# A two-layer decoder kernel: the router worked by token halves, the norm's root moved from the one-hots to the expert slots, and the first gather cut into chunks

## The chip, the cores and the metric

The kernel runs on one core of one Trainium2 chip. The metric is the device time of one execution in microseconds (us), and the time given is the median of three runs.

## The reference, cut to what matters

The model has two layers. Each adds a mixer (attention or a recurrence) to `x` and then a mixture of experts. There are 256 tokens of width 1024, 32 experts in 4 groups of 8, and an expert has 512 hidden columns. All is float32.

```
x += Mixer(RMSNorm(x))
x += HierMoE(RMSNorm(x)):
    g_logits = h @ wg_r + bg_r              # 4 groups, the best one is taken
    e_in     = (h @ we_r + be_r)[that group]
    top_v, top_i = top_k(e_in, 2)           # two experts of the group
    gate = softmax(g_logits)[best] * softmax(top_v)
    y[token] = sum over its two experts of gate * (silu(h @ w_gate[e]) * (h @ w_up[e])) @ w_down[e]
RMSNorm(x) = x * rsqrt(mean(x * x) + eps) * gain
```

## The kernel before, in words

The weights of the experts are read once per layer, 32 experts x 3 matrices x 2 MB. They pass through twelve places of 2 MB in the on-chip memory (`places`; a unit is what one place holds). All loads are issued by the SP queue in one fixed order. A load waits until the unit that was in its place is used up, which TensorE (PE) tells by the semaphore `unit_used`. `load_unit` (L366) does this for one unit and `load_matrices` (L385) for four at a time. Eight rounds ("quads") follow, with four experts each: a gate, an up and a down matrix, each of four units. In the first gate matrix of a layer (`QUARTERED`) a unit holds a quarter of the rows for all four experts, so that it is free after a quarter of the matrix. While PE goes through the end of the mixer and the router, SP has the first twelve units loaded and then has to wait.

Each engine's instructions are written out by hand in its own order. Around the router they are these:

- PE: the output projection (`project_out`, L1105), into it set the transposes of `x` (`turn_x`, L962). Token half 0 is transposed at once. The first columns of half 1 (`turn_x(pe, layer, 1, 0)`) wait for `added` to count VectorE's first addition for that half. The last four matmuls of the projection stand behind these transposes, and their end frees the last place for unit 5. Then `route_and_experts` (L1140) follows: two strips of partial logits, the logits, the copies of x into four PSUM banks (`start_sums`, which the experts' results are later added to), two matmuls that only keep the array at work (`keep_busy`), the ranks (how many earlier tokens chose the same expert), and `moe_pe`.
- VectorE (DVE): `finish_mixer` (L1539) adds the projection to `x`, half 0 whole and half 1 in two parts. It makes the mean squares, asks ScalarE for `exp(-0.5 ln v)`, and refines this by four small steps (`inverse_root`, L849). `route` (L1582) then makes the scores of both halves. Every pair of experts in a group is compared ("duels"), the two best of the best group are `picked`, and with the ranks one-hot matrices `sel` are made (`placed`, L790), which are multiplied by the root of each token (L799).
- ScalarE (ACT): `finish_mixer` (L1363) squares x, copies transposed x out of PSUM (`keep_xT`, L969), and takes the root (`take_root`, L861).

In `moe_pe` (L569) PE gathers the tokens of 4 experts x 32 slots by matmuls with `sel` (L577). Of the first quad, chunks 0 to 3 are gathered ahead of the gate matrix and chunks 4 to 7 behind its first quarter (`gather_rest`).

An engine takes its instructions in order. `turn(...)` and `and_wait(...)` put a wait for an instruction's own end behind it.

Of the kernel before, what the change touches and what calls it, by code (L numbers as in the profile page):

```python
# [92 lines left out]
ROOTS = ((2, 2), (20, 8), (28, 8), (2, 2), (2, 2), (44, 16), (44, 16), (44, 8), (2, 2))  # L93
# [47 lines left out]
def build(nc, t, where, const_width, stop_after=4):  # L141
    with ExitStack() as ctx:
# [118 lines left out]
        over_i = sb("over_i", [P, 2], I32)  # L261


        names = ["small_landed", "tables_landed", "sums_started", "in_half_landed", "begin_landed", "begin_second", "begin_third", "begin_fourth", "gains_landed", "xt_first_landed", "xt_second_landed", "xt_third_landed", "even_dims", "odd_dims", "gather_begun", "xT_begun", "half_landed", "x_first_landed", "x_second_landed", "first_landed", "pos_landed", "lb_landed", "router_landed", "masks0_landed", "masks_landed", "consts_landed", "filler_ready", "unit_used", "stored",
# [8 lines left out]
                 "strips", "strips_kept", "last_strips_kept", "logits_done", "group_max", "group_exp", "top_diff", "top_exp", "picked_ready", "ranks_done",  # L273
# [294 lines left out]

        def moe_pe(pe, layer, over, rnd):  # L569
# [4 lines left out]
            def gather_chunks(a, b, bank=None):  # L574
                for c in range(a, b):
                    for tc in range(TC):
                        mm = pe.matmul(psum[:, YB + c // 4 if bank is None else bank, (c % 4) * P:(c % 4 + 1) * P], x[:, tc, c * P:(c + 1) * P],  # L577
                                       sel[:, tc, :], start=tc == 0, stop=tc == TC - 1)
                return mm

            def gather(chunks=KC // 2):
                for half in range(2):
                    gather_chunks(4 * half, 4 * half + chunks).then_inc(m["gathered"], 1)

            def gather_rest():
                gather_chunks(4, 8).then_inc(m["gathered"], 1)
                pe.wait_ge(m["xT_ready"], 1)
# [20 lines left out]
            def matrix(i, matrix, out, inp, rows, width, halfway=lambda: None, quarterway=lambda: None):  # L608
# [7 lines left out]
                for c in range(rows - per if last else rows):  # L616
                    if c == rows // 2:
                        halfway()
                    if c == rows // 4:
                        quarterway()  # L620
# [18 lines left out]
            pe.wait_ge(m["sel_ready"], n17 + 1)  # L639
            if over:  # L640
                pe.wait_ge(m["y_ready"], 2 * n16)
# [1369 lines left out]
```

## Time and profile before

| | us |
|---|---|
| median of 3 runs | 1168.25 |
| lowest, highest | 1167.83, 1169.03 |
| profiled execution, its own time | 1166.55 |
| its span | 1164.8 |
| PE busy | 876.4 (75%) |
| DVE busy | 223.8 (19%) |
| ACT busy | 126.7 (11%) |
| DMA queue q1, share of the 16 engines | 91.0% |
| HBM read | 445.61 MB, 383 GB/s over the span |

The profiled execution took 1166.55 us, of which 1164.8 us is the span from its first to its last recorded event, so 1.75 us lie around the span. Layer 0's router stands at 157 to 180 us of the span and layer 1's at 722 to 745 us. Busy shares are averages over stages that have different limits.

### The profile page before, as it was taken

The page shows a single profiled execution, that of the slowest core. Times are in us where ns is not written, and L with a number is a line of the kernel's source. Part 1 is how long each engine was busy: PE and PEld are TensorE (multiplying, and loading weights), DVE is VectorE, ACT ScalarE, POOL GpSimd, SP SyncE. Part 2 cuts the span into 40 slices and gives each one's busy share as a digit, 9 for nine tenths or more (in the row PEclk, how much of TensorE's full clock was granted, in tenths as well). Part 3 has the DMA queues.
Part 4 walks back from the last instruction along what each step waited for, and adds up shares of the span by engine and source line. Part 5 has one row for each costly group of instructions (what it writes and reads, how often), then busy time and mean ns, then how long its engine had stood idle before and what let it go on. Part 6 is the DMA issues. An engine that isn't in the chain of part 4 may idle for free.

```text
span 1164.8 us, 11459 instructions
## 1 busy us (share of the span) xinstructions
PE 876.4 (75%) x5104; PEld 394.0 (34%) x5104; DVE 223.8 (19%) x470; ACT 126.7 (11%) x249; POOL 0.5 (0%) x5
## 2 busy tenths in 40 slices
PE   8999999747474738485899999977474747474776
PEld 7555554212121212121246655433131313131312
DVE  2732332010101010101127541410000101000001
ACT  3411311000000000000021431200000000000000
POOL 0000000000000000000000000000000000000000
PEclk9999999888888877777999999998787878788889
DMA  9776659999999999999996477899999999999997
GB/s 347 304 321 257 267 219 378 430 435 433 435 433 433 435 433 435 435 430 414 424 423 284 154 293 276 317 441 433 433 435 435 433 435 433 433 430 432 417 426 308
DMA packets 19637, 447.45 MB, mean 384 GB/s; under 512 B 2560, under 2 KB 2816, under 8 KB 5504
## 3 DMA queue, kind: packets, MB, share of 16 engines
q1 hardware_dynamic: 19584, 446.67, 91.0%
q8 instruction: 43, 0.70, 0.2%
q14 instruction: 10, 0.08, 0.0%
HBM read 445.61 MB, written 1.05 MB: 383 GB/s over the span
## 4 chain that ended last, share of the span: by engine, by line
DMA 56%; PE 42%; DVE 1%; another core or an unknown queue 1%; issue 0%; ACT 0%; SPq 0%; DVEq 0%
DMA places<-in_together 47%; PE psum L631 14%; PE psum L1016 11%; DMA places<-in_quarters 8%; PE psum L1117 5%; PE psum L1013 4%; PE psum L577 1%; PE psum L1029 1%; PE psum L1057 1%; PE psum L565 1%; DMA places<-in_w_in 0%; PE psum L1144 0%; PE psum L698 0%; PE psum L968 0%
## 5 line engine op out<-in xcount | busy, mean ns | idle before, releaser
L631 PE MATMUL psum<-places,mixed 128*32 128x512 f32 x3040 | 421.8, 707 | 276.3 <-DMA places<-in_together 249.2
L631 PEld LDWEIGHTS psum<-places,mixed 128*32 128x32 f32 x3040 | 110.4, 127 | 570.5 <-issue 448.7
L1016 PE MATMUL psum<-places 128*128 128x512 f32 x288 | 126.3, 593 | 0.0
L1016 PEld LDWEIGHTS psum<-places 128*128 128x128 f32 x288 | 53.6, 190 | 61.4 <-issue 61.2
L577 PEld LDWEIGHTS psum<-sel,x 128*128 128x128 f32 x528 | 60.4, 192 | 17.0 <-issue 15.1
L577 PE MATMUL psum<-sel,x 128*128 128x128 f32 x528 | 64.3, 279 | 1.7 <-DVE sel L799 1.7
L565 PE MATMUL psum<-y_sb,spread 128*128 128x512 f32 x128 | 59.6, 606 | 2.1 <-ACT y_sb L768 1.4
L820 DVE TENSOR_TENSOR sig<-psum,sig 128x512 f32<-128x512 f32 x16 | 11.1, 692 | 253.4 <-ACT sig L760 253.4
L823 DVE TENSOR_TENSOR mixed<-psum,sig 128x512 f32<-128x512 f32 x16 | 11.1, 692 | 245.4 <-PE psum L631 245.4
L833 DVE COPY y_sb<-psum 128x512 f32<-128x512 f32 x14 | 9.7, 692 | 180.2 <-PE psum L631 180.2
L762 ACT COPY mixed<-psum 128x512 f32<-128x512 f32 x16 | 9.4, 586 | 320.6 <-PE psum L675 320.6
L1013 PE MATMUL psum<-places 128*128 128x256 f32 x192 | 42.9, 381 | 0.0
L1013 PEld LDWEIGHTS psum<-places 128*128 128x128 f32 x192 | 36.1, 190 | 5.7 <-issue 1.0
L760 ACT ACTIVATE sig<-psum 128x512 f32<-128x512 f32 x16 | 9.6, 597 | 255.9 <-PE psum L631 255.9
L565 PEld LDWEIGHTS psum<-y_sb,spread 128*128 128x128 f32 x128 | 22.8, 189 | 38.6 <-issue 33.7
L768 ACT COPY y_sb<-psum 128x512 f32<-128x512 f32 x16 | 9.4, 586 | 209.2 <-PE psum L631 181.8
L1117 PE MATMUL psum<-places,y_sb 128*128 128x512 f32 x64 | 28.2, 594 | 0.7 <-ACT small L1396 0.7
L1117 PE MATMUL psum<-places 128*128 128x512 f32 x64 | 28.5, 592 | 0.0
L826 DVE TENSOR_TENSOR mixed<-psum,consts 128x512 f32<-128x512 f32 x32 | 21.9, 690 | 31.8 <-PE psum L577 31.8
L1117 PEld LDWEIGHTS psum<-places,y_sb 128*128 128x128 f32 x64 | 11.9, 190 | 14.8 <-issue 13.9
L1388 ACT ACTIVATE places<-psum,small 128x512 f32<-128x512 f32 x16 | 10.1, 684 | 57.7 <-PE psum L1016 53.6
L1117 PEld LDWEIGHTS psum<-places 128*128 128x128 f32 x64 | 11.8, 190 | 13.4 <-issue 13.4
(252 smaller groups left out, 505.4 us busy)
## 6 DMA issues: line engine op xcount, KB each, us to landing
places<-in_singles SPq DMA_DIRECT2D x32, 2048.0 KB, 10.1
places<-in_quarters SPq DMA_DIRECT2D x22, 2048.0 KB, 35.1
places<-in_w_in SPq DMA_DIRECT2D x12, 2048.0 KB, 26.7
places<-in_w_out SPq DMA_DIRECT2D x4, 2048.0 KB, 14.3
places<-in_quarters SPq DMA_DIRECT2D x4, 1024.0 KB, 45.6
places<-in_w_in SPq DMA_DIRECT2D x2, 1024.0 KB, 27.2
places<-in_w_in SPq DMA_DIRECT2D x3, 512.0 KB, 8.7
x<-in_x SPq DMA_DIRECT2D x2, 512.0 KB, 13.6
```

Of the source, the lines that this page charges most:

```text
L565: mm = pe.matmul(psum[:, ACC + 2 * n + tc, :], spread[:, tc, :], y_sb[:, 512 * n:512 * (n + 1)], start=False, stop=False, skip_group_check ...
L577: mm = pe.matmul(psum[:, YB + c // 4 if bank is None else bank, (c % 4) * P:(c % 4 + 1) * P], x[:, tc, c * P:(c + 1) * P], sel[:, tc, :], ...
L631: mm = pe.matmul(psum[slots, out + n, :], inp[:, c, slots], slot(layer, unit)[:, at + 512 * n:at + 512 * (n + 1)], start=c == 0, stop=c == ...
L820: turn(nc.vector.tensor_tensor(sig, psum[:, GATE, :], sig, ALU.mult))
L823: nc.vector.tensor_tensor(flat(act_h), psum[:, UP, :], sig, ALU.mult).then_inc(m["act_ready"], 1)
L826: nc.vector.tensor_tensor(xT[:, 4 * half:4 * half + 4, :], psum[:, 6 + half, :].rearrange("p (c s) -> p c s", s=P), gain_cols[:, 2 + layer ...
L1013: mm = pe.matmul(banks[:, m // 2, (m % 2) * SEQ:(m % 2 + 1) * SEQ], w[:, c, m * P:(m + 1) * P], hT[:, c, :], start=c == 0, stop=c == KC - 1)
L1016: mm = pe.matmul(banks[:, m, :], hT[:, c, m * P:(m + 1) * P], w[:, c, :], start=c == 0, stop=c == KC - 1)
L1029: mm = pe.matmul(psum[:, 4 + m, 0:SEQ], w[:, c, m * P:(m + 1) * P], hT[:, c, :], start=c == 0, stop=c == KC - 1)
L1057: mm = pe.matmul(banks[:, m, :], hT[:, c, m * P:(m + 1) * P], w[:, c, :], start=c == 0, stop=c == KC - 1)
L1117: return pe.matmul(psum[:, OUT_BANK[layer] + 2 * tc + n, :], mixT(half)[:, c, tc * P:(tc + 1) * P], w[:, c, 512 * n:512 * (n + 1)], start= ...
L1388: r = nc.scalar.activation(dst[:, tc * 512:(tc + 1) * 512], proj(g)[:, tc, :], function, scale=small[:, 2 + tc:3 + tc])
```

## The change

It does the following in both layers.

1. The root of token half 0 is asked for and refined right behind the first addition (`ask_root`, `refine_root` in DVE's `finish_mixer`), ahead of DVE's additions for half 1. ACT takes it behind its first `keep_xT`. The root of half 1 is asked for at the end and refined within the duels of half 0.
2. Scores, duels, picks, ranks and the first `sel` are made by token halves, each with a signal of its own.
3. `sel` is no longer multiplied by the roots. A matmul of `sel` with the roots gives one number per slot (`scale_slots`), ACT copies it to `slot_scale`, and it scales the sigmoid and both products of an expert.
4. The first gather goes by chunks: chunk 0 and chunk 1 ahead of the gate matrix, and the others ahead of its rows 2, 3 and 5 (`go_on_gathering`).
5. The matmuls for the largest expert count (`count_picked`) and all four `start_sums` go behind or into the first gate matrix, and the two `keep_busy` matmuls go.
6. `value_load` of the count on PE is put behind the loop over the quads.

The diff, cut to its core:

```
         def moe_pe(pe, layer, over, rnd):
+            def scale_slots(bank):
+                for tc in range(TC):
+                    mm = pe.matmul(psum[:, bank, SEQ:SEQ + 1], sel[:, tc, :], small[:, 2 + tc:3 + tc], start=tc == 0, stop=tc == TC - 1)
+                return mm
...
+            def begin_gather():
+                pe.wait_ge(S["sel_first"], layer + 1)
+                gather_some(0, 1, YB + 1, (0,))
+                gather_some(1, 2, YB, (0,))
+                pe.wait_ge(m["sel_ready"], 1)
+                gather_some(0, 1, YB + 1, (1,)).then_inc(S["gather_begun"], 1)
+                gather_some(1, 2, YB, (1,))
+                scale_slots(YB).then_inc(S["gather_begun"], 1)
+
+            def go_on_gathering(c):
+                begun = 3 * layer
+                if c == 0:
+                    pe.wait_ge(S["xT_begun"], begun + 1)
+                elif c == 1:
+                    pe.wait_ge(S["xT_begun"], begun + 2)
+                elif c == 2:
+                    gather_some(2, 4, YB + 1, range(TC)).then_inc(m["gathered"], 1)
+                    count_picked(pe)
+                    pe.wait_ge(m["xT_ready"], 1)
+                elif c == 3:
+                    gather_some(4, 6, YB, range(TC)).then_inc(S["gather_begun"], 1)
+                elif c == 4:
+                    pe.wait_ge(S["xT_begun"], begun + 3)
+                elif c == 5:
+                    gather_some(6, 8, YB + 1, range(TC)).then_inc(m["gathered"], 1)
+                elif c == 6:
+                    pe.wait_ge(m["xT_ready"], 2)
...
                 if first:
-                    pe.wait_ge(S["xT_begun"], layer + 1)
+                    matrix(0, 0, GATE, xT, KC, FF, each_chunk=go_on_gathering)
+                    start_sums(pe, layer, (0, 1, 2, 3))
+                    pe.wait_ge(S["route_ready"], layer + 1)
...
             def one_hots(quad):
-                placed(sel, quad)
-                nc.vector.tensor_tensor(sel, sel, small[:, 2:4].unsqueeze(2).broadcast_to([P, TC, P]),
-                                        ALU.mult).then_inc(m["sel_ready"], 1)
+                placed(sel, quad).then_inc(m["sel_ready"], 1)
...
-                nc.scalar.activation(sig, psum[:, GATE, :], ACT.Sigmoid).then_inc(m["sig_ready"], 1)
+                nc.scalar.activation(sig, psum[:, GATE, :], ACT.Sigmoid, scale=slot_scale).then_inc(m["sig_ready"], 1)
                 act.wait_ge(m["turned"], n16 + i + 1)
                 nc.scalar.copy(actT, psum[:, GATE, :].rearrange("p (c s) -> p c s", c=FC))
+                keep_scale(UP)
...
@@ TensorE, route_and_experts
-                logits(0)
+                logits(0).then_inc(S["logits_done"], 1)
                 pe.wait_ge(S["xT_third"], layer + 1)
                 strips(1, range(KC // 2, KC)).then_inc(S["strips"], 1)
-                start_sums(pe, layer, (0,))
                 pe.wait_ge(S["last_strips_kept"], layer + 1)
                 logits(1).then_inc(S["logits_done"], 1)
-                start_sums(pe, layer, (1, 2, 3)).then_inc(S["sums_started"], 1)
-                keep_busy(pe, 2, 7, ident, consts[:, 0:SEQ])
...
+                pe.wait_ge(S["picked_ready"], TC * layer + 1)
+                pe.matmul(psum[:, 4, 0:32], before, picked[:, 0, :], start=True, stop=True).then_inc(S["ranks_done"], 1)
+                pe.wait_ge(S["scores_read"], layer + 1)
+                pe.matmul(psum[:, 5, 0:32], ones[:, 0:P], picked[:, 0, :], start=True, stop=False)
+                pe.wait_ge(S["picked_ready"], TC * layer + 2)
+                pe.matmul(psum[:, 5, 0:32], before, picked[:, 1, :], start=False, stop=True).then_inc(S["ranks_done"], 1)
                 moe_pe(pe, layer, 0, 0)
@@ ScalarE, finish_mixer
                 keep_xT(layer, 0, slice(0, 2), nc.scalar.copy).then_inc(S["xT_first"], 1)
+                take_root(act, turn)
                 for half, signal in enumerate(("xT_second", "xT_third")):
@@ VectorE, finish_mixer
                 V.memset(rank.rearrange("p c e -> p (c e)"), 0.0)
+                ask_root(mean_square(dve, layer, 0), 2, 1)
+                refine_root(dve, turn)
                 dve.wait_ge(S["out_second"], layer + 1)
                 V.tensor_tensor(x[:, 1, 0:512], x[:, 1, 0:512], sums(1)[:, 0:512], ALU.add).then_inc(S["added"], 1)
...
                 keep_strips(0, V.tensor_copy).then_inc(S["strips_kept"], 1)
-                norm_root(dve, turn, 2 * layer + 1)
+                dve.wait_ge(S["squares"], SQUARES[2 * layer + 1])
+                turn(V.tensor_tensor(small[:, 1:2], small[:, 1:2], small[:, 7:8], ALU.add))
+                ask_root(mean_square(dve, layer, 1), 3, 1)
@@ VectorE, route
+                def duels(tc):
...
+                    turn(V.tensor_tensor(by_duel, ..., ALU.subtract))
+                    if tc == 0:
+                        refine_root(dve, turn)
+                    turn(V.tensor_tensor(by_row, by_row, ..., ALU.is_gt))
+                    turn(V.tensor_reduce(beaten_by[:, tc]..., by_duel, AX, ALU.add))
+                    turn(V.tensor_scalar(g_hot[:, tc], ..., 1.0, None, ALU.is_lt))
+                    and_wait(dve, V.scalar_tensor_tensor(by_group(picked[:, tc]), ...), S["picked_ready"], TC * layer + tc + 1)
...
+                scores(0)
+                duels(0)
+                scores(1)
+                V.memset(small[:, 60:61], 0.0).then_inc(S["scores_read"], 1)
+                duels(1)
+                place_first(0).then_inc(S["sel_first"], 1)
+                place_first(1).then_inc(M[layer]["sel_ready"], 1)
```

## Rows read from the trace of the kernel before

**Rows 1.** From the page, part 2: tenths of the clock and GB/s in 40 slices.

```profile
PEclk9999999888888877777999999998787878788889
GB/s 347 304 321 257 267 219 378 430 435 433 435 433 433 435 433 435 435 430 414 424 423 284 154 293 276 317 441 433 433 435 435 433 435 433 433 430 432 417 426 308
```

**Rows 2.** The chain that ended last: start us, us, what.

```profile
192.63 28.94 DMA places<-in_together
221.62 9.86 PE psum L631 x64
...
763.02 7.20 PE psum L631 x64
...
1097.94 8.59 PE psum L631 x64
```

**Rows 3.** The timeline of SP's queue, layer 0's router: start us, us, engine, line.

```profile
164.59 3.47 SPq L369 DMA_DIRECT2D places<-in_singles  x2
```

**Rows 4.** Stretches: length, busy per engine, then granted clock, DMA share, GB/s.

```profile
176.00:177.00 1.00, 1.00 (x13) 0.58 (x15) 0.00 (x0) 0.73 (x4) 0.00 (x0) 1.00 0.09 33
179.00:180.00 1.00, 1.00 (x12) 1.00 (x11) 0.93 (x4) 0.00 (x0) 0.00 (x0) 1.00 1.30 246
182.00:192.00 10.00, 10.00 (x100) 2.99 (x92) 0.69 (x1) 0.60 (x1) 0.00 (x0) 1.00 1.03 441
```

**Rows 5.** Timeline, end of layer 0's projection: start us, us, engine, line, operation.

```profile
159.84 0.69 DVE L1549 TENSOR_TENSOR x<-x,psum 128x512 f32<-128x512 f32 x1 [2.05 <-PE psum L1117]
160.72 1.01 ACT L974 COPY places<-psum 128x1024 f32<-128x1024 f32 x1 [1.90 <-PE psum L968]
...
162.24 0.60 PE L968 MATMUL psum<-consts,x 128*128 128x128 f32 x4
...
164.59 0.69 DVE L1551 TENSOR_TENSOR x<-x,psum 128x512 f32<-128x512 f32 x1 [4.06 <-PE psum L1117]
...
165.51 0.66 PE L968 MATMUL psum<-consts,x 128*128 128x128 f32 x4
...
166.20 0.59 ACT L974 COPY places<-psum 128x512 f32<-128x512 f32 x1 [0.17 <-PE psum L968]
...
167.16 0.16 DVE L856 TENSOR_TENSOR small<-small 128x2 f32<-128x2 f32 x1 [0.72 <-ACT small L867]
```

**Rows 6.** The same timeline, the router's scores, duels, picks and one-hots.

```profile
166.68 0.42 PE L1149 MATMUL psum<-both_strips,mixed 128*128 128x40 f32 x2
...
169.00 0.43 DVE L1602 SCALAR_TENSOR_TENSOR mixed<-psum,small,consts 128x40 f32<-128x40 f32 x2 [1.08 <-PE psum L1149]
...
169.46 0.82 DVE L1605 TENSOR_TENSOR mixed<-mixed 128x640 f32<-128x640 f32 x1
...
172.24 0.23 DVE L1611 SCALAR_TENSOR_TENSOR picked<-mixed 128x64 f32<-128x64 f32 x1
...
173.51 0.43 DVE L793 TENSOR_TENSOR sel<-consts,rank 128x256 f32<-128x256 f32 x1
```

**Rows 7.** The same timeline, PE's copies of x, gather and first expert matmuls.

```profile
168.72 2.82 PE L558 MATMUL psum<-x,consts 128*128 128x512 f32 x6
...
174.45 2.05 PE L577 MATMUL psum<-sel,x 128*128 128x128 f32 x16 [0.86 <-DVE sel L799]
...
176.44 1.92 PE L631 MATMUL psum<-places,mixed 128*32 128x512 f32 x16
...
180.27 12.22 PE L631 MATMUL psum<-places,mixed 128*32 128x512 f32 x112
```

**Rows 8.** Stretches of the expert stages, for the clock; columns as in Rows 4.

```profile
215.50:220.00 4.50, 0.00 (x0) 0.00 (x0) 0.00 (x0) 0.00 (x0) 0.00 (x0) 1.00 1.08 466
989.75:991.50 1.75, 0.00 (x0) 0.00 (x0) 1.41 (x3) 0.52 (x1) 0.00 (x0) 1.00 0.95 412
991.75:993.00 1.25, 0.00 (x0) 0.00 (x0) 0.00 (x0) 0.00 (x0) 0.00 (x0) 0.50 0.97 419
1149.00:1155.00 6.00, 3.98 (x30) 1.29 (x28) 0.00 (x0) 0.00 (x0) 0.00 (x0) 1.00 0.84 352
```

More of the change, by code:

```diff
@@ L606, in over_matrix, with matrix @@
                     mm.then_inc(m["used"], 1)
-            def matrix(i, matrix, out, inp, rows, width, halfway=lambda: None, quarterway=lambda: None):
+            def matrix(i, matrix, out, inp, rows, width, halfway=lambda: None, each_chunk=lambda c: None):
                 if over:
@@ L711, in moe_pe @@
             y_all = 2 * QUADS
+            count = pe.value_load(over_i[0:1, layer:layer + 1], min_val=0, max_val=SEQ)
             with pe.If(count > SLOTS):
@@ L771, in act_quad @@
                     nc.scalar.copy(y_sb[:, 512:1024], psum[:, YB + 1, :]).then_inc(m["y_ready"], 1)
-            keep_gathered(n17 + 1, first=not over)
+            if over:
+                keep_gathered(n17 + 1)
+            else:
+                begin_gathered()
             with act.Fori(0, QUADS if over else QUADS - 1) as i:
@@ L847, in build, with ask_root @@
         roots_asked, roots_taken = [], []
-        def inverse_root(dve, instruction, turn, col, count):
+        def ask_root(instruction, col, count):
             assert ROOTS[len(roots_asked)] == (col, count)
@@ L853, in inverse_root, with refine_root @@
             instruction.then_inc(S["root_in"], 1)
+        def refine_root(dve, turn):
+            col, count = roots_asked[-1]
             dve.wait_ge(S["root_out"], len(roots_asked))
@@ L859, in inverse_root @@
             turn(nc.vector.tensor_tensor(v, y, z, ALU.mult))
+        def inverse_root(dve, instruction, turn, col, count):
+            ask_root(instruction, col, count)
+            refine_root(dve, turn)
         def take_root(act, turn):
@@ new lines, in route, with scores @@
+                n_rows = SCORES // PER_GROUP
+                each = [P, n_rows, PER_GROUP, PER_GROUP]
+                by_group = lambda a: a.rearrange("p (g e) -> p g e", g=N_GROUPS)
+                def scores(tc):
+                    dve.wait_ge(S["logits_done"], TC * layer + tc + 1)
+                    turn(V.scalar_tensor_tensor(rt[:, 64 + tc * SCORES:64 + (tc + 1) * SCORES], psum[:, 4 + tc, SEQ:SEQ + SCORES],
+                                                small[:, 2 + tc:3 + tc], rb[:, layer, :], ALU.mult, ALU.add))
@@ new lines, in place_first @@
+                def place_first(tc):
+                    dve.wait_ge(S["ranks_done"], 3 * layer + tc + 1)
+                    turn(V.scalar_tensor_tensor(rank[:, tc, 0:32], psum[:, 4 + tc, 0:32], 1.0, picked[:, tc], ALU.add, ALU.mult))
+                    return V.tensor_tensor(sel[:, tc].rearrange("p (e s) -> p e s", e=TILE),
+                                           const("iota").unsqueeze(1).broadcast_to([P, TILE, SLOTS]),
+                                           rank[:, tc, 0:TILE].unsqueeze(2).broadcast_to([P, TILE, SLOTS]), ALU.is_equal)
```

156 lines of the change are left out of this document (73 added, 83 removed).

## The prediction

> **What bounds the kernel now.** Four views in turn. The page first: in 40 slices the DMA rate stands at 430 to 441 GB/s in slices 7 to 18 and 26 to 38 and falls to 154 between, so that the expert stages are bound by loads and the mixers are not [rows 1]. The chain of waits next: behind layer 0's first quad it goes over from PE to the four-unit load issued at 192.63 us, and from there each quad is a load with a short PE piece behind it [rows 2]. A load stream that never runs dry ends a fixed time after it begins. So the question is when it begins, and the stretches answer it: unit 5 is issued at 164.59 [rows 3], the DMA runs dry soon after 176.0 (33 GB/s in that us), and it is at work again in the us from 179.0 (246 GB/s), then at 441 GB/s throughout [rows 4]. What starts it is the end of the first quarter of the first gate matrix, which frees a place: 176.44 + 1.92 = 178.36 [rows 7]. I call this moment Q. Earlier than the dry point nothing is won, but Q may come some 2 us earlier with full gain. The last view is the timeline from the end of the projection to Q, and every edit is priced by what it does to Q. Layer 1 has the same instructions in the same order, so each term counts twice.
>
> **1. DVE's early root adds a wait (+1.57 us).** The root of half 0 needs ACT, and ACT takes it behind its first copy of transposed x, which starts at 160.72 [rows 5]. In the kernel before, a copy started at 166.20 and DVE's first refining step at 167.16, 0.96 later. This copy is 1.01 long where that one was 0.59, so the step comes 1.38 after 160.72, at 162.10 [rows 5]. Four steps at 0.20 (0.16 and the gap of the wait behind each) end at 162.89. DVE stands still from about 159.1 until then, and queued behind the waiting instruction is the first addition of half 1, which ran at 159.84 [rows 5]. It now runs 162.89 to 163.58. PE waits for it: a transposition follows an addition by 165.51 - 164.59 - 0.69 = 0.23, so this one begins at 163.81 instead of 162.24 [rows 5]. The rest of the projection stands behind it in PE's order, then the second addition, the strips, the logits, and in SP's queue units 5 and 6. All move by 1.57. The bounds are 0 (ACT takes the root before DVE would have added) and 1.9; I take 1.57, since each piece has a row. The dry point moves too, to 177.7, and still lies before Q.
>
> **2. The router by halves (a gain, with point 3).** The logits of half 0 end at 166.68 + 0.42 = 167.10, and now DVE may begin with them, 0.1 later, at 167.2 + 1.57 = 168.8; it was 169.00 for both halves [rows 6]. Then DVE is a chain. A pass over 640 elements takes 0.82 and one over 256 takes 0.43 [rows 6], so 320 elements take 0.50, and 0.53 with the gap. First half: scores 0.25 (half of 0.43, and the gap), three passes 1.60, the four root steps 0.79, the group's hot column 0.21 (the 0.16 of a small step [rows 5], a little over), picks 0.22 (0.23 for both halves [rows 6]): 3.07. Second half without the root: 2.28, and 0.10 for the memset (estimate from 0.16). Then a rank 0.22 and half of `sel`, 0.29 by the same line: 0.51. Sum 5.96, so the first half of `sel` stands at 174.75 and the second (0.22 + 0.32) at 175.3. Before, the whole stood at 174.4, with 0.42 of it for the multiplication by the roots that goes. The split pays a fixed 0.17 per instruction twice; this is why halves win so little. Bounds of this chain: 0.4 either way.
>
> **3. The gather by chunks.** 16 records of L577 take 2.05, 0.128 each, and PE did all 16 ahead of the gate matrix [rows 7]. Now from 174.81: four records (0.50), which end with the second half of `sel`; four more (0.50), and the four of `scale_slots` at weight-load pace (0.116 to 0.128, so 0.46 to 0.51), then 1.92 for the quarter. ACT's copies of chunk 0 and 1 fit under these. Q is 174.75 + 0.55 + 0.06 + 0.50 + 0.46 + 1.92 = 178.24, against 178.36: -0.12 per layer. Without point 1 it would be 176.7, -1.7.
>
> **4. Work put behind Q.** Between Q and the end of the up matrix PE has six rows of the gate matrix (0.86 each, 5.15), three gathers of 8 records (3.1), the counts (four records, 0.4), a wait for ACT's copy (0.45), `start_sums` (eight records; six took 2.82 [rows 7], so 3.7 at most and 3.44 at pace) and the up matrix (64 of the 112 records of 12.22 [rows 7], 6.98): 19.5, ending at 197.7 instead of 192.5. This frees units 16 to 19, whose load was issued at 192.63 [rows 2]. What hides it is the stream of units 12 to 15. Units 5 and 6 took from 164.59 to about 176.1, 11.5 us [rows 3, 4], of which 2 x 2.097 MB at 434 GB/s are 9.66; so a start costs 1.9. Four units end 1.9 + 19.3 = 21.2 us after Q, at 199.4. A load issued at 197.8 has data at 199.7 if the start costs 1.9 again, at 199.4 or before if its start is hidden. So +0.15 (0 to 0.5); the cover of 5 us is all but used up. The Trainium skill (DMA: Bandwidth & Descriptors, Anatomy of one DMA) puts the fixed cost mostly into the receipt at the end, not the start; by it this term is 0, and no row here separates the two.
>
> **5. PE's clock (+2.3 us, the largest term).** Before, PE had no pause in the router: six records of copies of x filled 168.72 to 171.5 [rows 7], then the keep-busy matmuls. All this goes or moves behind Q. What is left from the end of the last strips (167.7 + 1.57 = 169.3) to 174.8 is one logit, the rank of half 0, a sum and the rank of half 1: eight records, about 1.4 of 5.5 us. In the expert stages the granted clock falls after each long pause: it was still 1.00 after 4.5 us of silence at 220.0, but in another place already 0.50 at 2.0 us after 989.75 [rows 8]. It comes back only after some us of matmuls. The price of such a cold start (1.2 GHz for 2.4) has rows: 64 records of L631 took 7.20 warm, and 9.86 or 8.59 behind a pause [rows 2], so 2.7 and 1.4. Against a fall speaks 1149 to 1155, where PE was busy 3.98 of 6 us, with short pauses, at 1.00 [rows 8]; the new stretch has less than half that share. Bounds: 0 (no fall), 2.7. I take the fall and 2.3, nearer to 9.86 because the start is the same (gather and gate rows directly behind the pause) and because most first pieces of quads in the chain look like it. It all lies before Q: 3.4 of the 3.5 us from `sel` to Q are PE's. ACT, DVE and DMA have nothing that would take it back, as the queue is dry.
> The row of 1149 us shows short pauses without a fall. The Trainium skill (TensorE: Matmul & The Clock Gate, A second HAM failure mode) says that small idles between groups of matmuls can be frequent enough to make the clock go down and up. By it the fall comes; by that row alone it would not, and the sum below would be 4.6 smaller.
>
> **6. Edits at nothing.** `slot_scale` adds to ACT about 0.2 and to PE about 0.5 per quad, and DVE loses 0.42 of L799; in quads 1 to 7 the chain leads through the loads (28.94 for the first) with PE pieces of 7 to 10 between [rows 2]. In the last quad four quarter loads come 4.8 us apart after it, which covers 0.7. PE's `value_load` lies under the wait for the last up matrix. Without these covers it would be 0.7 per layer. The gates on DVE and the sigmoid's table load now stand behind ACT's last chunk; I estimate their ends at 188 and 187.3, before the up matrix needs either.
>
> **The sum.** Per layer -0.12 + 0.15 + 2.3 = +2.3; two layers +4.6. The profiled execution took 1166.55 (1164.8 of span and 1.75 around it), so 1171.2 on its scale; the median of three is 1.7 higher, 1168.25, so 1172.9. Own bounds per layer: -0.5 + 0 + 1.4 = 0.9 to 0.3 + 0.5 + 2.7 = 3.5, so 1170.1 to 1175.3.
>
> **Rivals.**
> - The clock stays up in both layers. For it: 1149 to 1155, and matmuls that break the pause three times. Against: their share is small. -0.12 + 0.15 per layer: 1168.3. Chance 0.17.
> - It falls in one layer only, since falls came between 2 and 5 us after a pause began: 1170.6. Chance 0.10.
> - Faster: the clock holds and DVE's wait costs nothing, because ACT takes the root before the projection needs DVE. Then point 1 is 0 and Q comes 1.7 earlier in each layer: 1164.9. For it: ACT stood idle 1.90 before that copy [rows 5]. Against: the copy's start at 160.72 against the addition at 159.84 [rows 5]. Chance 0.14.
> - Much slower: the loads run dry a second time. The up matrix ends later than 197.7 by more than 1 us, if the gathers between gate rows each wait for ACT's copy (four times 0.4), and each us beyond is a us of the end: 2.3 + 1.3 more per layer, 1175.5. It decides once units 16 to 19 are issued over 19.5 us after Q. Chance 0.09.
> - The forecast: 0.50.
>
> **How the numbers follow.** About 0.2% (2.3 us) is what a measurement of this kernel can tell. Slower: 0.48 of the forecast, 0.03 of the one-layer case, 0.09: 0.60. Same: 0.02, 0.07 and 0.14 of the case at 1168.3: 0.23. Faster: 0.03 and 0.14: 0.17. The range leaves out the faster case and the far end of the dry one: 1167.0 to 1175.5; the forecast's own is 1170.1 to 1175.3.
>
> **What would show it.** L1549's successor starts at 162.9 and L968's second group at 163.8 (point 1). The first half of `sel` ends near 174.8 if the clock doesn't enter (2). The granted clock reads 0.50 somewhere between 172 and 181, and the first quarter of the gate matrix ends near 180.6 instead of 178.36 (5). The DMA rate has no second hole near 199 (4). The prediction is wrong if the clock reads 1.00 throughout the router, or if the addition still runs at 159.8.

## The result, and the profile after

| | before | after |
|---|---|---|
| median, 5 runs each (us) | 1168.48 | 1177.44 |
| lowest, highest | 1167.83, 1169.53 | 1174.94, 1180.04 |
| profiled execution, its span | 1164.8 | 1175.6 |

The ratio is 1.0078, with a 95% interval of 1.0062 to 1.0095. That is 9.1 us slower, where 4.6 were forecast. The profiled execution of after took 1177.44 us.

Page of after, parts 2 and 3 (for queues: packets, MB, share of 16 engines) [rows 1]:

```profile
PEclk9999999978777777778999999898888787787889
GB/s 348 296 311 261 265 200 358 426 431 440 431 431 429 440 433 435 429 438 410 425 423 267 152 293 270 298 431 431 430 431 430 433 440 433 431 431 435 414 426 288
...
q8 instruction: 45, 0.74, 0.2%
```

The loads bound the expert stages as before. To see where the span grew (by 10.8 us as rounded in the table, by 10.9 unrounded), I cut both executions at the same events of each layer: A, the first transposition of x in the projection; `sel`, PE's first matmul with it; Q, the end of the first quarter of the first gate matrix; the issue of the first four-unit load (units 16 to 19); E, the start of the last down piece of the last quad. A0 and E0 are those of layer 0, A1 and E1 those of layer 1.

```
us               A0      A->sel       sel->Q      Q->issue     Q->E            E0->A1  E1->end
before           159.64  14.81/14.83  3.91/3.90   14.27/14.28  410.65/410.63   135.77  10.62
after            160.92  14.87/14.87  5.46/5.37   20.38/20.39  414.10/413.70   135.77  10.59
(layer 0 / layer 1)
```

The difference of the spans is 1.28 at the start + 3.12 up to Q (1.61 and 1.51) + 6.52 behind Q (3.45 and 3.07) - 0.03 = 10.89. The 1.28 is none of the change: A0 lay between 159.2 and 162.5 in the runs' kernels, which but for e8_code do the same up to there. To compare clock times of layer 0, take 1.28 from those of after.

Timeline of after, end of layer 0's projection (columns as in [rows 5]):

```profile
161.99 1.01 ACT L1033 COPY places<-psum 128x1024 f32<-128x1024 f32 x1 [1.90 <-PE psum L1027]
...
163.37 0.16 DVE L907 TENSOR_TENSOR small<-small 128x1 f32<-128x1 f32 x1 [3.10 <-ACT small L923]
...
164.14 0.69 DVE L1606 TENSOR_TENSOR x<-x,psum 128x512 f32<-128x512 f32 x1
...
164.89 0.66 PE L1027 MATMUL psum<-consts,x 128*128 128x128 f32 x4 [1.21 <-DVE x L1606]
```

DVE stands 3.10 us before its first refining step, and the addition behind it runs at 162.86 on the scale of before, where it was 159.84 [rows 5]. The forecast had 162.89.

The router's end and the first expert matmuls (against [rows 6, 7]):

```profile
172.94 0.41 PE L1225 MATMUL psum<-picked,consts 128*128 128x32 f32 x2 [1.76 <-DVE picked L1675]
...
175.24 0.63 PE L1229 MATMUL psum<-picked,consts 128*128 128x32 f32 x2 [1.29 <-DVE picked L1675]
175.44 0.29 DVE L1682 TENSOR_TENSOR sel<-consts,rank 128x128 f32<-128x128 f32 x1
175.79 2.08 PE L583 MATMUL psum<-sel,x 128*128 128x128 f32 x8
...
177.66 0.85 PE L590 MATMUL psum<-small,sel 128*128 128x1 f32 x4
178.44 2.81 PE L668 MATMUL psum<-places,mixed 128*32 128x512 f32 x16
```

Stretches of after (columns as in [rows 4]):

```profile
173.00:174.00 1.00, 0.93 (x4) 0.68 (x4) 0.92 (x4) 0.00 (x0) 0.00 (x0) 0.72 0.96 410
174.00:180.00 6.00, 4.76 (x22) 3.53 (x26) 3.31 (x15) 0.79 (x3) 0.00 (x0) 0.50 0.79 339
180.00:181.00 1.00, 1.00 (x12) 0.19 (x4) 0.00 (x0) 0.00 (x0) 0.00 (x0) 0.86 0.08 16
```

PE waits 1.76 and 1.29 us for DVE, the clock falls within the us from 173 and stays at 0.50 (1.2 GHz) until 180. Sixteen records of the quarter take 2.81 for 1.92 [rows 7], eight of the gather 2.08. By 180 the DMA is dry (16 GB/s), so all of it is lost.

Behind Q, PE in layer 0 (before, 112 records of 12.22 followed the gather, [rows 7]):

```profile
181.17 1.16 PE L583 MATMUL psum<-sel,x 128*128 128x128 f32 x8
182.17 0.31 PE L572 MATMUL psum<-picked,consts 128*128 128x32 f32 x2
182.31 0.39 PE L573 MATMUL psum<-picked,consts 128*128 128x32 f32 x2
183.05 1.06 PE L668 MATMUL psum<-places,mixed 128*32 128x512 f32 x8 [0.35 <-ACT mixed L778]
184.04 1.16 PE L583 MATMUL psum<-sel,x 128*128 128x128 f32 x8
185.13 1.92 PE L668 MATMUL psum<-places,mixed 128*32 128x512 f32 x16
186.98 1.16 PE L583 MATMUL psum<-sel,x 128*128 128x128 f32 x8
188.07 2.78 PE L668 MATMUL psum<-places,mixed 128*32 128x512 f32 x24
190.78 3.70 PE L559 MATMUL psum<-x,consts 128*128 128x512 f32 x8
194.42 7.07 PE L668 MATMUL psum<-places,mixed 128*32 128x512 f32 x64
```

The chunks of the gather (L583), the counts and the copies of x (L559) stand before the up matrix, whose end frees the places of units 16 to 19. Then SP's queue, and PE's first use of that load (against 192.63 and 221.62 in [rows 2]):

```profile
201.63 0.33 SPq L392 DMA_DIRECT2D places<-in_together  x1
```

```profile
226.47 3.21 PE L668 MATMUL psum<-places,mixed 128*32 128x512 f32 x28 [1.63 <-DMA places<-in_together]
```

The load is issued 20.38 after Q and is there at 45.22 after Q. Before, it was issued at 14.27 and there at 43.26 (221.62 - 178.36). The stream comes 2.0 us late. Layer 1: 44.5 for 43.0. The last thing to see is in quad 7 of layer 1, in the midst of an up matrix whose places had all landed:

```profile
1146.61 3.84 PE L668 MATMUL psum<-places,mixed 128*32 128x512 f32 x20 [3.85 <-issue]
```

"issue" means that nothing which the profile shows held PE. In the view of PE's waits (us in total, times, longest) these are, in after,

```profile
PE psum L668 <- issue: 4.7, 3, 3.8
```

and the kernel before has none of 0.8 us or more. What ends such a stop is taken up in the last section.

### The profile page after: what moved, and what is told of

Read it like the earlier page. It is cut to its first block, busy times and chain, and to the rows that moved or that the text cites. A ratio compares the mean times of both kernels' runs of the same rounds, so it can differ in the third digit from the quotient of the medians.

```text
span 1175.6 us, 11651 instructions
## 1 busy us (share of the span) xinstructions
PE 886.4 (75%) x5172; PEld 406.5 (35%) x5172; DVE 222.0 (19%) x478; ACT 130.5 (11%) x271; POOL 0.5 (0%) x5
## 4 chain that ended last, share of the span: by engine, by line
PE 49%; DMA 45%; another core or an unknown queue 3%; DVE 1%; issue 1%; ACT 1%; SPq 0%; DVEq 0%
DMA places<-in_together 36%; PE psum L668 18%; PE psum L1075 11%; PE psum L1176 4%; DMA places<-in_singles 4%; DMA places<-in_quarters 4%; PE psum L1072 4%; PE psum L583 2%; PE psum L566 2%; PE psum L1088 1%; PE psum L1116 1%; PE psum L559 1%; DMA places<-in_w_in 0%; PE psum L1027 0%
## 5 line engine op out<-in xcount | busy, mean ns | idle before, releaser
L1075 PEld LDWEIGHTS psum<-places 128*128 128x128 f32 x288 | 53.6, 190 | 61.4 <-issue 61.2
L583 PEld LDWEIGHTS psum<-sel,x 128*128 128x128 f32 x528 | 62.4, 196 | 18.5 <-issue 18.4
L583 PE MATMUL psum<-sel,x 128*128 128x128 f32 x528 | 67.2, 284 | 0.0
L867 DVE SCALAR_TENSOR_TENSOR sig<-psum,slot_scale,sig 128x512 f32<-128x512 f32 x16 | 12.0, 751 | 245.2 <-ACT sig L810 245.2
L870 DVE SCALAR_TENSOR_TENSOR mixed<-psum,slot_scale,sig 128x512 f32<-128x512 f32 x16 | 12.0, 751 | 243.5 <-PE psum L668 243.5
L1072 PE MATMUL psum<-places 128*128 128x256 f32 x192 | 42.9, 381 | 0.0
L1072 PEld LDWEIGHTS psum<-places 128*128 128x128 f32 x192 | 36.1, 190 | 5.7 <-issue 1.0
L810 ACT ACTIVATE sig<-psum,slot_scale 128x512 f32<-128x512 f32 x16 | 11.0, 687 | 242.5 <-PE psum L668 242.5
L1088 PE MATMUL psum<-places 128*128 128x256 f32 x64 | 15.5, 407 | 1.7 <-DMA places<-in_w_in 1.7
```

Of the source, the lines that this page charges most:

```text
L583: mm = pe.matmul(psum[:, bank, (c - a) * P:(c - a + 1) * P], x[:, tc, c * P:(c + 1) * P], sel[:, tc, :], start=tc == 0, stop=tc == TC - 1, ...
L867: turn(nc.vector.scalar_tensor_tensor(sig, psum[:, GATE, :], slot_scale, sig, ALU.mult, ALU.mult))
L870: nc.vector.scalar_tensor_tensor(flat(act_h), psum[:, UP, :], slot_scale, sig, ALU.mult, ALU.mult).then_inc(m["act_ready"], 1)
L1072: mm = pe.matmul(banks[:, m // 2, (m % 2) * SEQ:(m % 2 + 1) * SEQ], w[:, c, m * P:(m + 1) * P], hT[:, c, :], start=c == 0, stop=c == KC - 1)
L1075: mm = pe.matmul(banks[:, m, :], hT[:, c, m * P:(m + 1) * P], w[:, c, :], start=c == 0, stop=c == KC - 1)
L1088: mm = pe.matmul(psum[:, 4 + m, 0:SEQ], w[:, c, m * P:(m + 1) * P], hT[:, c, :], start=c == 0, stop=c == KC - 1)
```

## The experiments

The theory after the result: three losses, which are the clock's fall, the four-unit load too late, and something in the quads. The kernels called "after + ..." start from the changed kernel, the "before + ..." from the old one. Ratios are to before, with 95% intervals; 0.001 is 1.17 us.

**e1_value: after + `value_load` early.** The place of `value_load` was my first suspect for the stop.

```
+ (quad 0, behind wait route_ready)  counts.append(pe.value_load(over_i[0:1, layer:layer+1], ...))
- (behind the loop over quads)       count = pe.value_load(...)
```

> The changed kernel with one edit undone: TensorE reads the expert count right behind the copies of x of the first quad, not behind the loop over the quads. If the 3.9 us stop in the last quad of layer 1 (a wait for nothing that the profile shows) comes from reading the count shortly before the branch, the stop goes and the time falls by 1 to 2.5 us against the changed kernel, to about 1175.5. Rival: the stop belongs to the branch's own code and stays wherever the count is read; then the time is that of the changed kernel, 1177.4.

Measured 1177.80, ratio 1.0086 (1.0073 to 1.0099). The stop stays, 3.30 us long: `value_load` isn't it.

**e2_fill: after + matmuls that keep the array at work.**

```
  logits(1).then_inc(S["logits_done"], 1)
+ keep_busy(pe, 4, 7, ident, consts[:, 0:SEQ])
...
+ keep_busy(pe, 2, 7, ident, consts[:, 0:SEQ])
  pe.wait_ge(S["picked_ready"], TC * layer + 2)
```

> The changed kernel with fillers only: four filler matmuls behind the second logits and two ahead of the second rank, nothing else moved. If the clock's fall is a cost of its own, the granted clock reads 1.00 through both routers, the first quarter of the first gate matrix ends 1.7 to 2.5 us earlier against the first half of the one-hots, and the time falls by 3 to 5 us to about 1173.5. The load that starts 20.4 us after that quarter stays late, so the expert stages stay 1.5 to 1.9 us per layer longer than before. Rival: the matmuls for the ranks wait behind the fillers and give the gain back; then 1177 or more.

1172.32, ratio 1.0037 (1.0024 to 1.0050). The stretch that stood at 0.50 is warm:

```profile
174.00:180.00 6.00, 5.33 (x40) 3.31 (x40) 3.68 (x16) 0.78 (x3) 0.00 (x0) 1.00 0.88 374
```

`sel` to Q is 3.37 for 5.46 and 5.37. The clock is worth 2.1 and 2.0 us by these rows and 4.8 us by the ratios. Half of the loss is left. The long stop is gone too (the longest is 1.35), so part of the 4.8 may be the stop's and not the clock's.

**e3_sums: after + `start_sums` back behind logits(1).**

```
  logits(1).then_inc(S["logits_done"], 1)
+ start_sums(pe, layer, (0, 1, 2, 3))
...
- start_sums(pe, layer, (0, 1, 2, 3))     # behind the first gate matrix
```

> The changed kernel with the four copies of x back in the router, right behind the second logits. They fill the first pause (3.44 us) and leave the up matrix 3.44 us earlier. If late copies cost the load stream, both costs go: clock mostly up, and the four-unit load issued 17 us after the first quarter instead of 20.4, so the expert stages end as in the kernel before. Expected 1170 to 1172. Rival (the clock alone counts): same as the kernel with fillers, about 1173.5.

1170.09, ratio 1.0020 (1.0011 to 1.0029). The copies keep the clock at 1.00 too (`sel` to Q 3.37), and the load goes out 16.62 after Q and is there at 43.03. Against e2_fill 2.0 us come back: the price of the lateness, less what the stop costs, which is here again. Yet Q comes 0.49 earlier per layer than in before and the time is 2.3 us worse, so 3.3 us are lost elsewhere. The timeline of layer 1's quad 7 has a stop again, and the waits view sums them up:

```profile
PE psum L668 <- issue: 5.0, 3, 4.2
```

**e4_refine: after + `refine_root` for half 0 moved behind the additions and `keep_strips`.**

```
  ask_root(mean_square(dve, layer, 0), 2, 1)
- refine_root(dve, turn)
...
  keep_strips(0, V.tensor_copy).then_inc(S["strips_kept"], 1)
+ refine_root(dve, turn)
```

> The changed kernel with the refining steps of the first root behind the additions of half 1 and the copy of the first strips, so that VectorE no longer stands before the first addition of half 1. If the wait costs its 1.4 to 1.6 us per layer the time falls by 2.5 to 3.5 us to about 1174.5, and the transposes of half 1 follow the projection without a pause. Rival: the four steps now stand in front of the scores and the gain is smaller, 0.8 us per layer.

1177.27, ratio 1.0073 (1.0060 to 1.0086). A to `sel` is 13.43 for 14.87, so DVE's early wait costs 1.44 per layer (1.57 foretold). The cold clock eats half of it: `sel` to Q is 6.2. The time doesn't show the rest.

**e5_best: e3_sums + a filler before the second rank + e4's late refinement.** The diff is the sum of the ones above, with two `keep_busy` matmuls.

> The changed kernel with three things put right: the copies of x back behind the second logits, two fillers ahead of the second rank, and the first root refined behind the additions of half 1. From the runs so far: the one-hots stand 13.43 us after the first transposes (14.81 in the kernel before), the first quarter ends 3.37 later (3.91), so it comes 1.9 us per layer earlier than before; the four-unit load follows 16.6 after it, and the stream loses 0.8 per layer (2.6 in a layer with the stop in the last quad). Expected 1166 to 1168, so even with the kernel before or 1 to 2 us under it. Rival: an earlier first quarter meets the point where the loads run dry and nothing is won; 1169 to 1170.

1169.38, ratio 1.0019 (1.0010 to 1.0028). Q comes 1.4 us earlier per layer than in before (13.62 + 3.68 for 18.72), and nothing is won; the stop is 5.08 long. Something behind Q takes it.

**e6_late_copies: before + all `start_sums` behind the first gate matrix, router filled.**

```
- start_sums(pe, layer, (0,))
+ keep_busy(pe, 2, 7, ident, consts[:, 0:SEQ])
  pe.wait_ge(S["last_strips_kept"], layer + 1)
  logits(1).then_inc(S["logits_done"], 1)
- start_sums(pe, layer, (1, 2, 3)).then_inc(S["sums_started"], 1)
+ keep_busy(pe, 6, 7, ident, consts[:, 0:SEQ])
...
+ (behind matrix(i, 0, GATE, ...))  if first: start_sums(pe, layer, (0, 1, 2, 3))
```

> The kernel before with one edit of the change: all four copies of x behind the first gate matrix, their place in the router filled with matmuls that only keep the array at work. The first quarter stays at 3.91 behind the one-hots and the granted clock at 1.00. The up matrix and with it the four-unit load come 3.4 us later, 17.7 after the first quarter. If a load issued close to the end of the stream in front of it loses time, this alone makes the expert stages 0.8 to 1.5 us per layer longer: 1170 to 1171. Rival: there is still cover for 17.7 (the four units end 21.2 after the quarter), nothing is lost, 1168.

1168.21, ratio 1.0000 (0.9991 to 1.0009). Its four-unit load, issued at 195.95, 18.05 after its Q of 177.90, is used at 43.0 as before:

```profile
220.90 5.36 PE L631 MATMUL psum<-places,mixed 128*32 128x512 f32 x48 [2.15 <-DMA places<-in_together]
```

Moving the copies is free up to there.

**e7_single_loads: after + units 16 to 19 loaded one by one** (`TOGETHER = range(20, 84)`).

> The changed kernel with units 16 to 19 of each layer loaded by four transfers of 2 MB, not by one of 8 MB; the rest is unchanged, and they are still issued at the same point, 20.4 us after the first quarter. If the 1.5 to 1.9 us that the stream loses there are the start of one large transfer on an almost empty queue, four small ones start faster and the expert stages get 1 us per layer shorter: 1175.5. Rival: any transfer issued there starts as late; 1177.4, no change.

1178.82, ratio 1.0099 (1.0083 to 1.0114): the rival holds. The four single loads go out 20.25 to 21.58 after Q (180.09), no earlier than the one load of after (20.38), for all four places come free only with the end of the up matrix. PE still waits for one of them at 45.17:

```profile
225.26 7.05 PE L668 MATMUL psum<-places,mixed 128*32 128x512 f32 x58 [0.59 <-DMA places<-in_singles]
```

In layer 0 PE has the next four-unit load 64.6 after Q, as in after, where before has it at 62.7. So the stream is as late with small loads as with a large one: it is the lateness of the issue that costs, not the size of the load. Q to E is 413.45 and 416.30 for 414.10 and 413.70; the 2.6 more in layer 1 have no shown cause.

**e8_code: before + 34 small matmuls at the program's start.**

```
+ for _ in range(34):
+     pe.matmul(psum[:, 0, 0:32], spread[:, 0, :], spread[:, 1, 0:32], start=True, stop=True, ...)
```

> The kernel before with 34 tiny matmuls more on TensorE (32 columns) at the start of the program, while it waits for the first weights: nothing else changes but that all later TensorE code lies further on, by as much as the changed kernel has more of it. If the 3 to 4 us stop in layer 1's last up matrix comes from where that code lies, it appears here too, and the last quarter of layer 1 ends up to 1.5 us later: 1168 to 1170. Rival: the stop comes from something in the changed kernel's last quad itself; none here, 1168.0.

1181.75, ratio 1.0114 (1.0097 to 1.0130). They didn't hide under the first load, as both forecasts had assumed: 68 records took 14.4 us, 0.21 each, and A0 moved from 159.64 to 174.12. The medians differ by 13.6 us, less than A0 moved, so no loss shows behind A0; but A0 alone varied by 3 us in the other kernels, and this run can't settle a loss of 1 or 2. Q to E in its profile grew by 1.24 and 1.49 and I took this for a cost of code at first; the median doesn't bear it out, and one execution of a kernel can't settle 1 us: e16_wide_in_quads, about 1 us slower than before, shows 1.6 more in layer 1 and nothing in layer 0.

**e9_later: before + copies late + three wide matmuls behind them.** The lateness of after with hardly any other instruction.

```
  (e6_late_copies' edits, the fillers as five 128x512 matmuls)
+ for _ in range(3):      # behind start_sums
+     pe.matmul(psum[:, UP, :], ident, x[:, 0, 0:512], start=True, stop=True, ...)
```

> The kernel before with all start_sums behind the first gate matrix and three more 512-wide matmuls behind them, so that the four-unit load of units 16 to 19 is issued about 20.5 us after Q, as in the kernel after; the router's gaps are filled with five 512-wide matmuls, so Q stays and the clock is 1.00. Almost no other instruction is added. Theory 'late load': the lateness alone costs the stream 1.5 to 1.9 us per layer (Q to the end of the stage 410.6 -> 412.3), time about 1171.5. Rival 'only the grown code': the load may be this late for nothing, Q to the end stays at 410.7, time about 1168.3.

1171.13, ratio 1.0022 (1.0012 to 1.0032): +2.6 us. Timeline, first four-unit load's issue and its use (Q is 179.89):

```profile
200.52 0.33 SPq L391 DMA_DIRECT2D places<-in_together  x1
```

```profile
225.21 3.21 PE L631 MATMUL psum<-places,mixed 128*32 128x512 f32 x28 [1.88 <-DMA places<-in_together]
```

Issue to use is 24.69, in after 24.84 (226.47 - 201.63), where four units at 434 GB/s are 19.3. So the load must be issued 43.26 - 24.8 = 18.4 us after Q at the latest. 18.05 costs nothing (e6), 20.6 costs 2.1 in layer 0. The 18.4 is good to about 1 us: in layer 1 issue to use is 23.2 here and 24.1 in after, and the landings are 0.9 and 1.5 late; the longest among the kernels with so late a load is 25.6 (e4_refine, layer 1).

**e10_code_in_quads: before + 34 tiny matmuls in quads 1 to 7.**

```
  spread_back(pe, tc)   # both
+ for _ in range(5 if i == 1 else 2):
+     pe.matmul(psum[0:8, YB + 1, 0:8], ident[:, 0:8], consts[:, 0:8], start=True, stop=True, ...)
```

> The kernel before with 34 tiny matmuls more on PE (8 columns by 8), 17 per layer, spread over quads 1 to 7 behind the gate matrices, where PE has room before a load; each a few hundredths of a us. Nothing else is changed. Theory 'grown code': more instructions have to be fetched, so there are about 45 packets in the instruction queue for 43, and somewhere late in a layer PE stands 2 to 4 us with nothing that the profile shows; Q to the end of the stage grows by 1.2 to 1.5 us in at least one layer, time 1169.5 to 1171. Rival 'late load only': the matmuls hide under the loads, 410.6 stays, time 1168.3.

1168.57, ratio 1.0005 (0.9996 to 1.0014). As many records as `scale_slots` has, in other places, and no loss that can be measured. The instruction queue has 44 packets where 45 were expected, and the longest stop is 1.42.

**e11_no_slot_scale: e5_best without `slot_scale`.**

```
- scale_slots(...), keep_scale(...), scale=slot_scale
- nc.vector.scalar_tensor_tensor(sig, psum[:, GATE, :], slot_scale, sig, ALU.mult, ALU.mult)
+ nc.vector.tensor_tensor(sig, psum[:, GATE, :], sig, ALU.mult)
+ V.tensor_scalar(sel[:, tc], sel[:, tc], small[:, 2 + tc:3 + tc], None, ALU.mult)
```

> The kernel after with start_sums back behind the logits, two fillers before the second rank, the roots refined late, and slot_scale taken out: sel is multiplied by the roots half by half, as in the kernel before. So no code is added in the quads. Theory (late load, clock and code are all the loss): sel to Q about 3.7, Q to the four-unit load 16.6, Q to the end 410.7 in both layers, Q some 1.2 us earlier than before per layer: time about 1166. Rival: the earlier Q brings nothing (the loads are dry before it anyway or DVE eats it), 1168.3 or more.

1167.17, ratio 0.9989 (0.9979 to 0.9999): 3.5 us better than e5_best, and the one version that beats both kernels, if only just. No stop above 1 us. Its Q comes 1.14 us earlier per layer than in before, 2.3 in all, of which 1.3 arrive (the interval leaves 0.1 to 2.5).

**e12_cold: before + copies late, no fillers.** The clock alone, in the old kernel.

```
- start_sums(pe, layer, (0,))
- start_sums(pe, layer, (1, 2, 3)).then_inc(S["sums_started"], 1)
- keep_busy(pe, 2, 7, ident, consts[:, 0:SEQ])
+ (behind matrix(i, 0, GATE, ...))  if first: start_sums(pe, layer, (0, 1, 2, 3))
```

> The kernel before with all start_sums behind the first gate matrix and no fillers at all in the router: PE's clock alone, in the old kernel, with fewer instructions than before. Theory 'clock': the granted clock falls to 0.50 in the router, sel to Q grows from 3.9 to about 6.0 in each layer, Q to the four-unit load is 18.1 and costs nothing: time about 1172.4. Rival (the clock falls only where the work is cut into chunks): 1168.3.

1171.73, ratio 1.0032 (1.0022 to 1.0042): +3.7 us. Stretch and gather of this kernel (2.05 for the same records in [rows 7]):

```profile
174.00:180.00 6.00, 4.58 (x20) 4.45 (x21) 3.52 (x15) 0.55 (x2) 0.00 (x0) 0.50 0.82 352
```

```profile
177.33 3.78 PE L577 MATMUL psum<-sel,x 128*128 128x128 f32 x16 [0.46 <-DVE sel L801]
```

`sel` to Q is 6.70 and 5.89 for 3.9. The late copies cost nothing by e6_late_copies, so the 3.7 are the clock's. No edit of the sequence is needed for the fall, only PE's silence, here a pause of 3.62 us before the first rank.

**e13_pe_scale_only: e11 + PE's `scale_slots` alone**, the results unread.

```
+ mm = pe.matmul(psum[:, bank, SEQ:SEQ+1], sel[:, tc, :], small[:, 2+tc:3+tc], ...)   # two per quad
```

> e11_no_slot_scale (sel multiplied by the roots on DVE) with only PE's matmuls of scale_slots put back, their results unread: 68 records more in PE's code, in the places where the kernel after has them; ACT's and DVE's work as in e11. Theory 'PE's instructions': the stop of PE for nothing that the profile shows comes back (3 to 5 us in quad 7 of layer 1), 45 packets in the instruction queue for 43, time about 1170, as e5_best. Rival 'ACT and DVE': the loss of e5_best against e11 lies in the slot_scale copies and scaled products; no long stop, time about 1167.5.

1170.51, ratio 1.0017 (1.0008 to 1.0026): 3.3 us worse than e11, as e5_best. The stop is back:

```profile
1140.54 3.76 PE L668 MATMUL psum<-places,mixed 128*32 128x512 f32 x20 [4.99 <-issue]
```

ACT's and DVE's parts of `slot_scale` are cleared.

**e14_after_no_scale: after + `slot_scale` taken out.** The diff is e11's part alone.

> The kernel after with only slot_scale taken out: sel multiplied by the roots on DVE half by half (+0.4 us in the router per layer), no scale_slots (-0.5 before Q). Clock fall, DVE's wait and the late four-unit load stay. If slot_scale is one of the terms of the loss and they add up, about 3.5 us come back: 1174 (Q to the end about 412.5 in both layers for 414). Rival: the loss behind Q is all lateness, and the time stays at 1177.

1176.48, ratio 1.0070 (1.0056 to 1.0084): 1.0 us less than after where 3.5 were expected. Q to E is 413.54 and 413.13 for 414.10 and 413.70, and no stop is above 0.9. So in after itself the term is about 1 us by the medians, but with five runs each the two intervals leave anything up to 3.5. That it is smaller beside the other two losses is likely and not shown.

**e15_pe_scale_narrow: e13 with narrow weights** (`sel[:, tc, 0:8]` for `sel[:, tc, :]`).

> e13_pe_scale_only with the same 68 records in the same places, but narrow: 8 columns of sel for 128, so that the weight loads are short. The results are unread. Theory 'fetch' (the number and place of the instructions is what costs): 45 packets in the instruction queue, a stop of 3 to 5 us in quad 7 of layer 1, time 1170.5 as e13. Rival 'time' (PE's 0.5 us more per quad costs): time 1167.2 as e11, and e10's tiny matmuls cost nothing for the same reason.

1168.65, ratio 1.0006 (0.9997 to 1.0015), between e11 and e13. The stop doesn't care about the width:

```profile
1136.91 3.64 PE L668 MATMUL psum<-places,mixed 128*32 128x512 f32 x20 [4.66 <-issue]
```

**e16_wide_in_quads: e10 with full weights** (`ident` for `ident[:, 0:8]`).

> e10_code_in_quads (the kernel before with 34 matmuls more on PE) with full weight loads of 128 columns in the same places: about 0.13 us per record for 0.06, 0.5 us per quad. Theory 'fetch': as e10, since the instructions are the same in number: 1168.6. Rival 'time': the 0.5 us per quad costs as in e13, 1170 to 1171.5.

1169.34, ratio 1.0008 (0.9999 to 1.0017), no stop above 0.7. Neither theory of e15 and e16 takes all. The stop comes with the instructions' number and place, not with their time: it is there with narrow weights (e15) and not with as many wide ones elsewhere (e16). Of e13's 3.3 us by the ratios, 2.0 stay with narrow weights and 1.3 go with them, each with about 1.5 of uncertainty; this split stays open.

## Why the prediction was wrong in size and right in direction

Of the steps as they were put:

- **Step 1, DVE's early root (+1.57).** Right: 1.44 by e4_refine.
- **Steps 2 and 3 (-0.12 with step 1).** Nearly: with a warm clock A to Q is 14.86 + 3.37 = 18.23 for 18.72 (e2_fill, e3_sums), so -0.49 per layer.
- **Step 5, the clock (+2.3 per layer).** Right in mechanism and size: 2.1 and 2.0 by rows, 4.8 us for both layers by the ratio of after and e2_fill, 3.7 in the old kernel (e12_cold). The 0.7 between the rows and the 4.8 may be the long stop, which e2_fill lacks; then e2_fill against e3_sums, where it is back, makes the lateness 0.7 too cheap, and 2.7 is near the 2.6 of e9_later. The Trainium skill (TensorE: Matmul & The Clock Gate, A second HAM failure mode) says that frequent small idles between groups of matmuls make the clock drop and recover. This trace agrees so far: PE worked in single ranks with pauses between, the clock fell within the us from 173, just behind the pause of 1.76, read 0.50 through the next one of 1.29, and came back on its own in the first quarter. It is one fall and one return per layer, not a series.
- **Step 4, the work put behind Q (+0.15, 0 to 0.5).** This is the term that was mis-sized; it measured 1.0 to 1.3 per layer. The load is issued 20.38 after Q for 19.5: 0.4 of it is lost between Q and the copies (9.5 for 9.1, with one wait of 0.35 for ACT), 0.2 in the copies, 0.1 in the up matrix and 0.1 from its last matmul to the issue. The larger error is the reserve. I took a start of 1.9 us and so a landing 21.2 after issue; from issue to use it is 24.8 (24.1 in layer 1), and single loads in the same place are no faster (e7_single_loads). Even the forecast's own 19.5 lies past the 18.4 that the runs allow. The rival "much slower" named a second dry point and put it at 19.5; its condition, four waits for ACT, did not come, so the lateness is its hit and the reason is not. Its price of 1.3 per layer fits: 2.0 us for both layers by e2_fill against e3_sums, 2.6 by e9_later. The Trainium skill (DMA: Bandwidth & Descriptors, Anatomy of one DMA, written of another issue path) has a fixed 2.0 us and bytes at 436 GB/s, which makes an estimate of 21.2 us for these 8.39 MB. The runs show 23.2 to 25.6 from issue to use, with the queue still moving 410 GB/s in the us of the issue in after, so that the load also waits for what stands ahead of it; the measurement decides.
- **Step 6, `slot_scale` at nothing.** Wrong. It costs 3.3 us where loads and clock are in order (e13_pe_scale_only against e11_no_slot_scale), and about 1.0 in after (anything up to 3.5). I had asked only whether PE's 0.5 us fit under a load. In the old kernel they do (e16_wide_in_quads is 0.4 us above e10_code_in_quads, inside the noise); in the changed one 2.0 of the 3.3 stay when the records are made short (e15_pe_scale_narrow). Not asked was what more instructions do to PE's supply of them. That the place of `value_load` costs nothing was right (e1_value).

The sum by these terms: -1.0 for Q, +4.8 clock, +2.0 lateness, +3.3 PE's instructions = +9.1, as measured. The forecast of 4.6 was 1.7 short on the lateness and 3.3 on the instructions, and 0.7 too high on Q; the clock was hit within 0.2. But the first three make it close by construction (after, e2 and e3 in turn leave 3.3 for the rest); only the 3.3 of e13 against e11 is independent. And e14 gives 1.0 instead of 3.3 for the last one; if that holds, no single split of the 9.1 is the right one. Of the 6.5 us behind Q in the profile, 3.5 are the later landing (2.0 and 1.5) and 1.1 the scaling by e14; the remaining 1.9 of this one execution have no shown cause.

## What to carry to other kernels

A queue that is never dry has a latest issue time, not just an order: before work is moved ahead of what frees a place, measure issue to use of a load that goes out late in the stream, and keep that much before the moment of its use. Matmuls that only fill a pause were not free to remove here (3.7 and 4.8 us): look at the granted clock wherever PE is left with single matmuls between DVE's steps. If an edit adds PE instructions to every round of a stage, undo it by itself, even where each round has room.

## What the runs showed that I had not expected

PE can stop for 3.3 to 5.1 us in the midst of a matrix with all its operands there. It happened in quad 7 of layer 1 in the six kernels with 45 packets in the instruction queue that also have `scale_slots` (after, e1, e3, e4, e5, e7) and in e13 and e15, which have its matmuls and 45 packets too; kernels with 43 or 44 packets had 1.4 at most, and so had e8 with 45. e2_fill has `scale_slots` and 24 records more than after, but 44 packets and no long stop. Around the stop, the DMA view of 25 us shows (queue, packets, MB, share), in after from 1126 to 1151

```profile
q8 instruction: 4, 0.07, 1.1%
```

and in before for the same part of the layer (1118 to 1143)

```profile
q8 instruction: 2, 0.03, 0.5%
```

The times of the single packets in the traces say what PE waits for. In after PE stops at 1142.77; a packet of the instruction queue begins 1.36 us later and takes 1.07, and 1.42 us behind its end PE goes on, at 1146.61. It is so each time: all runs together have 18 stops of 0.7 us or more with nothing that the profile shows, the 1.42 of e10 among them, and every one ends 1.30 to 1.52 us behind the end of an instruction packet, where the packets themselves are about 6 us apart. So these are, by their timing, waits for instructions. In the eight long stops the packet begins only 0.7 to 2.6 us after PE has stopped, in the short ones 1.2 to 1.8 us before. Why it comes so late in those eight kernels, and whether the full load stream holds it up, no run shows.
